# Four combinations of a scaled input: five GpSimd operations in place of four VectorE operations, in four gated stages

## The chip, the cores and the metric

The kernel runs on one core of one Trainium2 chip. The metric is the device time of one execution in microseconds. The kernel before took 2028.01 us (median of 3 runs, 2027.89 to 2028.39).

## The reference, cut to what matters

The program is two transformer blocks in float32 over 512 tokens of width 1024. The first has a SwiGLU feed-forward, a mixer (window attention beside a pooling branch) and a second SwiGLU. The second block has two layers, each a mixer followed by a convolutional feed-forward. The change touches only the first half (gate and up projections) of the four feed-forwards:

```
h = h + 0.5 * swiglu(rms_norm(h, g), w_gate, w_up, w_down)    # twice: stages up1, up2
u, v = split(rms_norm(h, w) @ w_up)                           # twice: stages up3, up4
c = conv_b + sum_j conv_w[j] * shift(u, 2 - j)
y = (gelu(c) * v) @ w_down
```

Each of these projections is 1024 by 2 x 2816.

## The kernel before, in words

Activations are kept with features on the 128 partitions and the 512 tokens along the free axis; `h` is 8 chunks of 128x512. Every float32 matrix product is made of three TensorE matmuls (`product`, L1285 to L1287): each factor is split into a rounded part (`hi`) and the remainder (`lo`), and hi*hi, hi*lo and lo*hi are summed in PSUM. ScalarE makes the `hi` parts by a copy (L1766 for weights, L1994 for weights of a summed pair, L2030 for `xq`), VectorE the `lo` parts by a subtraction (L1794, L2598).

A stage up1 to up4 works through 22 pairs of weight tiles (f = 0 to 21), each pair a gate tile and an up tile, double-buffered in `raw`, `w_hi` and `w_lo`. The first PLAIN = 6 pairs are computed plainly, 48 matmuls of 512 columns each. From f = 6 on each product is put together from seven products of halved size, a Strassen-like scheme, which takes sums of the weight quarters (`w_sum`, L2535 to L2545) and seven combinations of the quarters of the scaled input: `xq`, seven pieces of 128x1024 float32 for the values and seven for their `hi` parts. This input has to be ready when pair 6 begins. It is made while VectorE also evacuates the plain pairs:

- `scaled_quarters` (L2580, after pair 1): eight instructions of VectorE, 128x512 each, write the four quarters x11, x21, x12, x22 = h * norm weight * rstd.
- `sum_quarters`: four instructions of VectorE on 128x1024. Part 0 (L2588, L2589) makes s1 = x22 - x21 and s2 = -s1 - x11, part 1 (L2591, L2592) overwrites x21 by x11 - x21 and makes s4 = -x12 - s2. The last one raises `xq_sum`. In up1 and up2 all four follow `scaled_quarters` at once; in up3 and up4 part 0 stands in pair 2 behind the convolution taps (L2606, L2609) and part 1 in pair 3 ahead of that pair's `rest_weights`.
- `round_quarters` (ScalarE, L2030) waits for `xq_sum`. Its group 0 stands in ScalarE's order of pair 3 behind the weights of pair 5 and ahead of `silu(3)`, group 1 behind `silu(3)`, groups 2 and 3 in pair 4.
- `rest_quarters` (VectorE, L2598): group 0 at the end of pair 3, groups 1 and 2 in pair 4, group 3 in pair 5. TensorE waits for each in pair 6 (`xq_ready`, L1576 to L1595).

Each engine executes its own instructions in the order in which they are written. VectorE's order in pair f (`plain_dve`) is: evacuate gate and up from PSUM (L2666 or L2669, and L2670), weights' remainder of pair f + 2 (L1794), in up3 and up4 the taps, the product with the activated gate (L2564), which waits for ScalarE's `silu`, and then what belongs to the special pairs. Pair 3 ends with the weight sums of pair 6 and `rest_quarters(0)`. TensorE can start pair f only when pair f - 2 is evacuated and the weights of f are split.

GpSimd's program (L3003 on) has nothing to compute in up1 and up2. In up3 and up4 it issues the transfers that add up weight quarters: `copy_gate` (L3036) for pair 6 early in the stage, then for each pair from 6 on the accumulating transfers L3027 (waits for the pair's weights) and L3029 (waits for the copy).

Of the kernel before, what the change touches and what calls it, by code (L numbers as in the profile page):

```python
# [9 lines left out]
ALU = mybir.AluOpType  # L10
# [23 lines left out]
SEVEN = ("up1", "up2", "up3", "up4")  # L34
# [106 lines left out]
def wait(eng, sem, count):  # L141

    if not isinstance(count, int) or count > 0:
        eng.wait_ge(sem, count)


def chunk(t, m, width=T):

    if isinstance(m, int):
        return t[:, m * width:(m + 1) * width]  # L150
    return t[:, bass.ds(m * width, width)]


def column(t, c):
    return t[:, c:c + 1] if isinstance(c, int) else t[:, bass.ds(c, 1)]
# [18 lines left out]
def build(nc, x_t, vecs, weights, mixer_consts, pool_tab, small_consts, pool_w, sinks, rel_bias, out_t, scratch, skew, stop=None):  # L174
# [4 lines left out]
    with ExitStack() as ctx:  # L179
# [4 lines left out]
        def at(name, shape, dt, offset):  # L184
            return nc.alloc_sbuf_tensor_at(name, shape, dt, offset=offset)
# [6 lines left out]
        def sem(name):  # L192
            return ctx.enter_context(nc.semaphore(name))
# [48 lines left out]
        xq32 = at("xq32", [P, 14 * XQ], F32, act_at + 32 * ROOM)  # L242
# [151 lines left out]
        hg_turned = sem("hg_turned")  # L394
        hg_gated = sem("hg_gated")
        xq_sum, xq_hi_ready, xq_ready = sem("xq_sum"), sem("xq_hi_ready"), sem("xq_ready")
        seven_done = sem("seven_done")
        seven_kept = sem("seven_kept")
        w_summed = sem("w_summed")
# [729 lines left out]
        def own_act(f):  # L1129
            return chunk(act32, (16 + f) % KF)  # L1130
# [7 lines left out]
        def quad(t, n, count=1):  # L1138
            return t[:, n * QUAD:(n + count) * QUAD]
# [4 lines left out]
        def xq_lo_at(n, count=1):  # L1144
            return slice((7 + n) * XQ, (7 + n + count) * XQ)
# [642 lines left out]
        def rest_weights(eng, q, i, per):  # L1788

            slot = q % 2  # L1790
            wait(eng, hi_rounded, whole_rounds(q) + per * i)
            n = PAIR_TILES[q] * P
            w = slice(slot * PAIR, slot * PAIR + n)
            eng.tensor_tensor(w_lo[:, w], raw[:, w], w_hi[:, w].bitcast(F32), ALU.subtract).then_inc(lo_rounded, 1)  # L1794
# [477 lines left out]
        def _(eng):  # L2272
            steps = [0]

            def link(ins):

                steps[0] += 1
                ins.then_inc(dve_step, 1)
                eng.wait_ge(dve_step, steps[0])
# [267 lines left out]
            def rest_sum(st, f, c):  # L2547

                eng.wait_ge(w_sum_hi_ready, 3 * seven_index(st, f) + c + 1)
                eng.tensor_tensor(quad(w_sum_lo, c), sum_at(st, f, c), quad(w_sum_hi, c).bitcast(F32), ALU.subtract)\  # L2550
                    .then_inc(w_sum_lo_ready, 1)
# [21 lines left out]
            def scaled_quarters(st):  # L2573

                for k in range(KD):
                    own = chunk(h, k).rearrange("p (a t) -> p a t", a=2)
                    by = rstd[:, :].rearrange("p (a t) -> p a t", a=2)
                    c, j = 2 * (k // 4), k % 4
                    to = xq32[:, xq_lo_at(c, 2)].rearrange("p (a k t) -> p a k t", a=2, k=KD // 2)[:, :, j, :]
                    ins = eng.scalar_tensor_tensor(to, own, column(vec, SEVEN_NORM[SEVEN.index(st.name)] + k), by,  # L2580
                                                   ALU.mult, ALU.mult)
                link(ins)

            def sum_quarters(st, part):

                x11, x21, x12, x22, s2, s1, s4 = (xq32[:, xq_lo_at(c)] for c in range(7))
                if part == 0:
                    link(eng.tensor_tensor(s1, x22, x21, ALU.subtract))  # L2588
                    link(eng.scalar_tensor_tensor(s2, s1, -1.0, x11, ALU.mult, ALU.subtract))  # L2589
                else:  # L2590
                    eng.tensor_tensor(x21, x11, x21, ALU.subtract)  # L2591
                    eng.scalar_tensor_tensor(s4, x12, -1.0, s2, ALU.mult, ALU.subtract).then_inc(xq_sum, 1)  # L2592

            def rest_quarters(st, j):

# [63 lines left out]
            def plain_dve(st, f, f0):  # L2659

                conv = st.evac == "conv"
                b = 5 if f == 0 else 2 * ((st.g0 + f) % 2)
                eng.wait_ge(pair_done, st.q0 + f + 1)
                if conv:
                    wait(eng, gate_ready, f0 + f)
                    eng.tensor_tensor(shifted[:, 2:], bank(b), rstd[:, :], ALU.mult).then_inc(u_ready, 1)  # L2666
                else:
                    wait(eng, gated_ready, f0 + f)
                    eng.tensor_tensor(gate[:, :], bank(b), rstd[:, :], ALU.mult).then_inc(gate_ready, 1)  # L2669
                eng.tensor_tensor(own_act(f), bank(b + 1), rstd[:, :], ALU.mult).then_inc(evacuated, 1)  # L2670
                if f == 3 and conv:
                    sum_quarters(st, 1)
                if 0 < f < PLAIN - 2:
                    rest_weights(eng, st.q0 + f + 2, 0, 0)
                if f == PLAIN - 2:
                    rest_weights(eng, st.q0 + PLAIN, 0, 0)
                    rest_sum(st, PLAIN, 0)
                if f == 1:
                    gated_product(st, 0, f0)
                if conv and f < PLAIN - 1:  # L2680
                    other_taps(st, f)
                if f == 1:
                    scaled_quarters(st)
                    if not conv:
                        sum_quarters(st, 0)
                        sum_quarters(st, 1)
                if f == 2 and conv:
                    sum_quarters(st, 0)
                if f == PLAIN - 2:
                    rest_quarters(st, 1)  # L2690
                if 0 < f < PLAIN - 1:
                    gated_product(st, f, f0)
                if f == PLAIN - 3:
                    sum_pair(st, PLAIN)
                    fourth_sum(st, PLAIN)
                    rest_quarters(st, 0)
                if f == PLAIN - 2:
                    rest_quarters(st, 2)
                    rest_sum(st, PLAIN, 1)
                if f == PLAIN - 1:  # L2700
                    rest_quarters(st, 3)
                    rest_sum(st, PLAIN, 2)
# [72 lines left out]
            for st in stages:  # L2775
                if st.name in IN:
                    a = IN.index(st.name)
# [47 lines left out]
                if st.name in OUT:  # L2825
                    a = OUT.index(st.name)
# [177 lines left out]
        def _(eng):  # L3004
# [30 lines left out]
            def copy_gate(st, f):  # L3035
                eng.dma_start(sum_at(st, f, 1), quad(weights[st.name][f], 0)).then_inc(copy_landed[f % 2], 16)  # L3036

            for st in stages:
                if st.name in ("up3", "up4"):
                    for f in range(PLAIN, KF):  # L3040
                        sums_by_transfer(st, f)
                if st.name == "in3":
                    eng.wait_ge(pair_done, st.q0)
                    eng.dma_start(mask3[:, :], mixer_consts[2][:, 2 * T:2 * T + P]).then_inc(const_landed, 16)
                    stream_gpsimd(eng)
                if st.name in IN:

                    eng.wait_ge(pair_done, st.q0)
                    a = IN.index(st.name)
                    eng.dma_start(mconst[:, :], mixer_consts[a]).then_inc(const_landed, 16)  # L3050
                    if a == 0:
                        eng.memset(swapped[:, :], 0.0).then_inc(swap_clear, 1)
                        eng.dma_start(ptab[:, :], pool_tab).then_inc(tab_landed, 16)
                        eng.dma_start(pw[:, :], pool_w).then_inc(tab_landed, 16)
                if st.name == "in1":
                    pool_gpsimd(eng)
                if st.name in HALVED and BARRIERS[st.name]["kind"] == "post":
                    bar, n = BARRIERS[st.name], HALVED.index(st.name)
                    tail = bar["x_index"] is None
                    for hf, m in tiles_in_order(st):  # L3060
                        if tail and (m % 2 if hf else m % 3 == 2):
                            continue
                        if hf:
                            eng.wait_ge(scaled_ready, bar["h0"] - 8 + m + 1)
                        else:
                            eng.wait_ge(a_scaled, KD * (n - 1) + m + 1)
                        own = half_chunk(h, m, hf)
                        done = tail_pool if tail else h_ready if hf else a_h
                        eng.tensor_tensor(own, own, (tail_product(m, hf) if tail else (gate, gated)[m % 2])[:, cols(hf)], ALU.add)\
                            .then_inc(done, 1)  # L3070
# [115 lines left out]
```

## Time and profile before

| what | value |
|---|---|
| median of 3 runs | 2028.01 us |
| the profiled execution's own time | 2028.04 us |
| its span, first to last instruction | 2026.3 us |
| TensorE busy | 2005.3 us, 99% |
| VectorE busy | 1459.0 us, 72% |
| ScalarE busy | 986.8 us, 49% |
| GpSimd busy | 244.1 us, 12% |
| granted TensorE clock | full in every slice |

The profile comes from one execution. Shares are of the span; a stage is seen in the timeline, where each row has a start, a duration, the engine, line, operation, output and inputs. In brackets stands how long the engine had been idle before the instruction, and what ended that.

### The profile page before, as it was taken

Reading aid. Unit: us, or ns where it says so; the run is one execution under the profiler, and the core shown is the slowest. Engines: PE = TensorE matmul, PEld = TensorE weight load, DVE = VectorE, ACT = ScalarE, POOL = GpSimd, SP = SyncE. Lnnn points to the kernel's source line nnn. Section 1 sums busy time; section 2 is a strip of 40 time slices with the busy share of each in tenths; the row PEclk is TensorE's granted clock in tenths of the full one; section 3 lists DMA queues with packets and bytes.
Section 4 is the critical chain, followed back from the end, with each engine's and each line's share of the span. In section 5 each row is a group of like instructions: output and inputs, shape, how many; then the busy total and the mean of one; then the engine's idle time right before and its main releaser. Section 6 shows DMA issues by size and latency. Waiting matters only on the chain.

```text
span 2026.3 us, 32634 instructions
## 1 busy us (share of the span) xinstructions
PE 2005.3 (99%) x12670; PEld 1757.3 (87%) x12670; DVE 1459.0 (72%) x2427; ACT 986.8 (49%) x1607; POOL 244.1 (12%) x266
## 2 busy tenths in 40 slices
PE   9999999999999999999999999999999999999998
PEld 7899988778899988988788899988877788999887
DVE  7888833786798863587778988933657779988733
ACT  5555622254445552453455555622557754555522
POOL 0000000500000000000002122000536520221001
PEclk9999999999999999999999999999999999999999
DMA  8322233312223223321321566333256624666232
GB/s 257 125 105 105 79 101 112 132 56 93 86 105 105 99 87 98 106 104 63 94 84 68 164 185 182 105 102 112 106 136 172 162 73 135 172 183 172 87 99 70
DMA packets 90141, 236.99 MB, mean 117 GB/s; under 512 B 47728, under 2 KB 51104, under 8 KB 73616
## 3 DMA queue, kind: packets, MB, share of 16 engines
q1 hardware_dynamic: 72896, 184.04, 27.6%
q0 software_dynamic: 14768, 37.49, 8.4%
q10 hardware_dynamic: 2336, 13.52, 1.9%
q8 instruction: 96, 1.57, 0.3%
q14 instruction: 45, 0.37, 0.1%
HBM read 211.86 MB, written 7.38 MB: 108 GB/s over the span
## 4 chain that ended last, share of the span: by engine, by line
PE 90%; DVE 6%; ACT 1%; issue 1%; DMA 0%; POOL 0%; SPq 0%; DVEq 0%
PE ps L1285 29%; PE ps L1286 28%; PE ps L1287 28%; DVE act L2556 1%; PE ps L512 1%; PE ps L525 1%; PE ps L736 1%; PE ps L718 1%; DVE w_lo L1784 1%; PE ps L703 1%; DVE w_lo L1794 1%; DVE w_sum_lo L2550 0%; DMA raw<-in_w_up 0%; PE ps L1272 0%; PE ps L1307 0%
## 5 line engine op out<-in xcount | busy, mean ns | idle before, releaser
L1794 DVE TENSOR_TENSOR w_lo<-raw,w_hi 128x2048 fp32r<-128x2048 f32 (+3 forms) x144 | 287.6, 1997 | 154.3 <-ACT w_hi L1766 146.3
L1285 PE MATMUL ps<-act,w_hi 128*128 128x512 f32 (+1 forms) x1026 | 376.3, 367 | 2.7 <-DVE w_lo L1794 1.6
L1286 PE MATMUL ps<-act,w_hi 128*128 128x512 f32 (+1 forms) x1026 | 372.0, 363 | 0.0
L1287 PE MATMUL ps<-act,w_lo 128*128 128x512 f32 (+1 forms) x1026 | 371.9, 362 | 0.0
L1285 PE MATMUL ps<-xq,w_hi 128*128 128x256 f32 x1024 | 290.6, 284 | 2.9 <-DVE up L2731 1.6
L1287 PE MATMUL ps<-xq,w_lo 128*128 128x256 f32 x1024 | 289.9, 283 | 0.0
L1286 PE MATMUL ps<-xq,w_hi 128*128 128x256 f32 x1024 | 289.9, 283 | 0.0
L1285 PEld LDWEIGHTS ps<-act,w_hi 128*128 128x128 f32 x1026 | 193.5, 189 | 40.4 <-issue 7.9
L1285 PE MATMUL ps<-xq,w_sum_hi 128*128 128x256 f32 x768 | 218.0, 284 | 1.7 <-ACT prod L2010 1.2
L1287 PEld LDWEIGHTS ps<-act,w_lo 128*128 128x128 f32 x1026 | 193.6, 189 | 30.0
L1286 PEld LDWEIGHTS ps<-act,w_hi 128*128 128x128 f32 x1026 | 193.7, 189 | 28.9
L1286 PE MATMUL ps<-xq,w_sum_hi 128*128 128x256 f32 x768 | 217.4, 283 | 0.0
L1287 PE MATMUL ps<-xq,w_sum_lo 128*128 128x256 f32 x768 | 217.4, 283 | 0.0
L1285 PEld LDWEIGHTS ps<-xq,w_hi 128*128 128x128 f32 x1024 | 196.6, 192 | 4.3 <-DVE up L2731 2.0
L1766 ACT ACTIVATE w_hi<-raw 128x1536 fp32r<-128x1536 f32 (+3 forms) x80 | 119.1, 1489 | 163.6 <-PE ps L1287 159.3
L1286 PEld LDWEIGHTS ps<-xq,w_hi 128*128 128x128 f32 x1024 | 196.6, 192 | 0.2
L1287 PEld LDWEIGHTS ps<-xq,w_lo 128*128 128x128 f32 x1024 | 196.6, 192 | 0.0
L1285 PE MATMUL ps<-x_split,w_hi 128*128 128x512 f32 (+1 forms) x400 | 161.3, 403 | 0.0
L1287 PE MATMUL ps<-x_split,w_lo 128*128 128x512 f32 (+1 forms) x400 | 153.0, 383 | 0.0
L1286 PE MATMUL ps<-x_split,w_hi 128*128 128x512 f32 (+1 forms) x400 | 152.9, 382 | 0.0
L1285 PEld LDWEIGHTS ps<-xq,w_sum_hi 128*128 128x128 f32 x768 | 147.4, 192 | 2.6 <-ACT prod L2010 1.6
L1287 PEld LDWEIGHTS ps<-xq,w_sum_lo 128*128 128x128 f32 x768 | 147.5, 192 | 0.0
(301 smaller groups left out, 3977.3 us busy)
## 6 DMA issues: line engine op xcount, KB each, us to landing
raw<-in_w_up SPq DMA_DIRECT2D x87, 1024.0 KB, 4.8
raw<-in_w_down SPq DMA_DIRECT2D x29, 768.0 KB, 4.2
raw<-in_w_in SPq DMA_DIRECT2D x20, 1024.0 KB, 4.7
raw<-in_w_down SPq DMA_DIRECT2D x29, 640.0 KB, 3.8
raw<-in_w_out SPq DMA_DIRECT2D x8, 1024.0 KB, 4.8
w_sum<-in_w_up POOLq DMA_DIRECT2D x32, 256.0 KB, 4.4
raw<-raw POOLq DMA_DIRECT2D x32, 256.0 KB, 3.3
w_sum_odd<-in_w_up POOLq DMA_DIRECT2D x32, 256.0 KB, 4.3
```

Source lines behind the costliest of these rows:

```text
L512: ins = pe.matmul(score_bank(i, hh)[:, at_:at_ + w], ring[rows, qs:qs + P], ring[rows, ks:ks + w], start=True, stop=True)
L525: ins = pe.matmul(pair_bank(c)[64 * hh:64 * hh + 64, n * P:(n + 1) * P], v_tok[:, vc:vc + 64], turned_at(u)[:, hh, at_ + j * P:at_ + (j + ...
L703: ins = pe.transpose(bank(TURN_BANK + hh)[:, to:to + P], exps_at(a, u, hh)[:, at_ + j * P:at_ + (j + 1) * P], ident)
L718: ins = pe.matmul(bank(SCORE_BANK + hh)[:, to:to + w], tile_at(a, ROPED[a][1 + c])[rows, n * P:(n + 1) * P], keys[rows, lo * P:(hi + 1) * ...
L736: ins = pe.matmul(pair_bank(c)[64 * hh:64 * hh + 64, n * P:(n + 1) * P], g_vtok[a][:, vc:vc + 64], g_turned_at(a, u)[:, hh, to:to + P], st ...
L1285: pe.matmul(own, hi, rhs_hi, start=start, stop=False, skip_group_check=more)
L1286: pe.matmul(own, hi, rhs_lo, start=False, stop=False, skip_group_check=more)
L1287: return pe.matmul(own, lo, rhs_hi, start=False, stop=stop, skip_group_check=more)
L1766: eng.activation(w_hi[:, w], raw[:, w], ACT.Copy).then_inc(hi_rounded, 1)
L1784: ins = eng.tensor_tensor(w_lo[:, w], raw[:, w], w_hi[:, w].bitcast(F32), ALU.subtract)
L1794: eng.tensor_tensor(w_lo[:, w], raw[:, w], w_hi[:, w].bitcast(F32), ALU.subtract).then_inc(lo_rounded, 1)
L2556: eng.tensor_tensor(chunk(act, act_lo(f)), own_act(f), chunk(act, act_hi(f)).bitcast(F32), ALU.subtract)\
```

## The change

`sum_quarters` leaves VectorE and becomes GpSimd's. The algebra is rearranged: s1 = x22 - x21, s4 = s1 + x11, x21 = x11 - x21, s2 = -s4, s4 = s4 - x12, five instructions on 128x1024 where there were four. Two semaphores are new: `xq_scaled`, raised by the last of the eight scaling instructions, which GpSimd waits for, and `xq_step`, which orders its own five. `xq_sum` is raised by the last as before, so ScalarE's waits are unchanged. In GpSimd's program the five stand ahead of the transfers of up3 and up4.

```diff
@@ scaled_quarters, sum_quarters (VectorE)
-                link(ins)
-
-            def sum_quarters(st, part):
-
-                x11, x21, x12, x22, s2, s1, s4 = (xq32[:, xq_lo_at(c)] for c in range(7))
-                if part == 0:
-                    link(eng.tensor_tensor(s1, x22, x21, ALU.subtract))
-                    link(eng.scalar_tensor_tensor(s2, s1, -1.0, x11, ALU.mult, ALU.subtract))
-                else:
-                    eng.tensor_tensor(x21, x11, x21, ALU.subtract)
-                    eng.scalar_tensor_tensor(s4, x12, -1.0, s2, ALU.mult, ALU.subtract).then_inc(xq_sum, 1)
+                ins.then_inc(xq_scaled, 1)
@@ plain_dve (VectorE)
-                if f == 3 and conv:
-                    sum_quarters(st, 1)
...
-                    if not conv:
-                        sum_quarters(st, 0)
-                        sum_quarters(st, 1)
-                if f == 2 and conv:
-                    sum_quarters(st, 0)
@@ the GpSimd program
+            def sum_quarters(st):
+
+                a = SEVEN.index(st.name)
+                x11, x21, x12, x22, s2, s1, s4 = (xq32[:, xq_lo_at(c)] for c in range(7))
+                eng.wait_ge(xq_scaled, a + 1)
+                eng.tensor_tensor(s1, x22, x21, ALU.subtract).then_inc(xq_step, 1)
+                eng.wait_ge(xq_step, 3 * a + 1)
+                eng.tensor_tensor(s4, s1, x11, ALU.add).then_inc(xq_step, 1)
+                eng.tensor_tensor(x21, x11, x21, ALU.subtract)
+                eng.wait_ge(xq_step, 3 * a + 2)
+                eng.tensor_scalar(s2, s4, -1.0, None, ALU.mult).then_inc(xq_step, 1)
+                eng.wait_ge(xq_step, 3 * a + 3)
+                eng.tensor_tensor(s4, s4, x12, ALU.subtract).then_inc(xq_sum, 1)
+
             for st in stages:
+                if st.name in SEVEN:
+                    sum_quarters(st)
                 if st.name in ("up3", "up4"):
                     for f in range(PLAIN, KF):
                         sums_by_transfer(st, f)
```

## Rows read from the trace of the kernel before

**Rows 1.** The page's first part: engine, busy us, share of the span, instructions.
```profile
PE 2005.3 (99%) x12670; PEld 1757.3 (87%) x12670; DVE 1459.0 (72%) x2427; ACT 986.8 (49%) x1607; POOL 244.1 (12%) x266
```
**Rows 2.** Timeline of TensorE in pair 6 and 7: start us, us, engine, line.
```profile
82.68 0.39 PE L1285 MATMUL ps<-xq,w_sum_hi 128*128 128x256 f32 x1 [0.59 <-ACT prod L2010]
1151.44 0.36 PE L1285 MATMUL ps<-xq,w_hi 128*128 128x256 f32 x1 [0.59 <-DVE w_lo L1794]
1157.67 0.39 PE L1285 MATMUL ps<-xq,w_sum_hi 128*128 128x256 f32 x1 [0.25 <-ACT up L2010]
1160.99 0.39 PE L1285 MATMUL ps<-xq,w_hi 128*128 128x256 f32 x1 [0.20 <-DVE up L2640]
1738.50 0.36 PE L1285 MATMUL ps<-xq,w_hi 128*128 128x256 f32 x1 [0.39 <-DVE w_lo L1794]
```
**Rows 3.** One line's instructions, minimum, median, maximum ns, first and last start.
```profile
L2588 DVE TENSOR_TENSOR xq<-xq x4: 1217/1222/1226, 43.5 to 1703.5; 128x1024 f32<-128x1024 f32 x4
```
**Rows 4.** Timeline of VectorE in up1.
```profile
38.10 5.38 DVE L2580 SCALAR_TENSOR_TENSOR xq<-h,vec,rstd 128x512 f32<-128x512 f32 x8
...
55.19 2.29 DVE L1794 TENSOR_TENSOR w_lo<-raw,w_hi 128x2048 fp32r<-128x2048 f32 x1 [0.72 <-ACT w_hi L1766]
...
59.57 0.69 DVE L2535 TENSOR_TENSOR w_sum<-raw 128x512 f32<-128x512 f32 x1 [1.36 <-DMA raw<-in_w_up]
...
74.94 0.69 DVE L2669 TENSOR_TENSOR gate<-ps,rstd 128x512 f32<-128x512 f32 x1 [0.37 <-PE ps L1287]
```
**Rows 5.** Timeline of ScalarE in up1.
```profile
55.06 1.90 ACT L2030 ACTIVATE xq<-xq 128x2048 fp32r<-128x2048 f32 x1
```
**Rows 6.** Timeline of VectorE in up2.
```profile
524.86 5.38 DVE L2580 SCALAR_TENSOR_TENSOR xq<-h,vec,rstd 128x512 f32<-128x512 f32 x8
...
543.81 2.29 DVE L1794 TENSOR_TENSOR w_lo<-raw,w_hi 128x2048 fp32r<-128x2048 f32 x1 [0.72 <-ACT w_hi L1766]
...
563.56 0.69 DVE L2669 TENSOR_TENSOR gate<-ps,rstd 128x512 f32<-128x512 f32 x1 [0.36 <-PE ps L1287]
```
**Rows 7.** Timeline of VectorE in up3.
```profile
1105.55 5.39 DVE L2580 SCALAR_TENSOR_TENSOR xq<-h,vec,rstd 128x512 f32<-128x512 f32 x8
...
1112.78 2.28 DVE L1794 TENSOR_TENSOR w_lo<-raw,w_hi 128x2048 fp32r<-128x2048 f32 x1
...
1127.44 0.69 DVE L2564 TENSOR_TENSOR act<-gated,act 128x512 f32<-128x512 f32 x1 [0.70 <-ACT gated L1983]
```
**Rows 8.** GpSimd's lines with SBUF inputs: minimum, median, maximum ns.
```profile
L3069 POOL TENSOR_TENSOR h<-h,gate x29: 720/915/1010, 1061.8 to 2019.2; 128x256 f32<-128x256 f32 x29
...
L424 POOL TENSOR_TENSOR pool_e<-csum x4: 1039/1288/1537, 369.2 to 388.8; 128x513 f32<-128x513 f32 x4
...
L427 POOL TENSOR_TENSOR pool_e<-pool_e,ptab x4: 1293/1306/1630, 370.3 to 390.4; 128x513 f32<-128x513 f32 x4
...
L630 POOL TENSOR_SCALAR biases<-biases x16: 1487/1650/2317, 1450.0 to 1597.2; 128x512 f32<-128x512 f32 x16
```
**Rows 9.** Timeline where GpSimd and VectorE compute side by side.
```profile
393.69 1.62 POOL L431 TENSOR_TENSOR proj<-gated,proj 128x512 f32<-128x512 f32 x1
394.08 1.78 DVE L828 TENSOR_TENSOR up<-proj,mconst 128x512 f32<-128x512 f32 x1
...
399.00 0.68 DVE L828 TENSOR_TENSOR up<-proj,mconst 128x512 f32<-128x512 f32 x1
...
1457.79 1.49 POOL L630 TENSOR_SCALAR biases<-biases 128x512 f32<-128x512 f32 x1 [1.89 <-DMA biases<-skew]
...
1458.52 0.69 DVE L1784 TENSOR_TENSOR w_lo<-raw,w_hi 128x512 fp32r<-128x512 f32 x1
```
**Rows 10.** Timeline of GpSimd in up3.
```profile
1091.22 0.58 POOL L3036 DMA_DIRECT2D w_sum<-in_w_up  x1 [8.45 <-DVE ssum L2471]
1120.31 0.91 POOL L3027 DMA_DIRECT2D raw<-raw  x1 [28.51 <-DMA raw<-in_w_up]
```

More of the change, by code:

```diff
@@ L396, in build @@
         xq_sum, xq_hi_ready, xq_ready = sem("xq_sum"), sem("xq_hi_ready"), sem("xq_ready")
+        xq_scaled, xq_step = sem("xq_scaled"), sem("xq_step")
         seven_done = sem("seven_done")
```

## The prediction

> **What bounds the kernel now.** I read the page first, then TensorE's timeline through the four stages, then the other engines' timelines around each hole in it. TensorE is busy 99% of the span [rows 1]: nothing is gained except where it idles, and every microsecond that something else makes it wait is added whole. Up to the start of pair 6 its matmuls in these stages stand back to back apart from the statistics at the start. The holes come in pairs 6 and 7, where the seven-product scheme begins. In up1 TensorE waits at 82.68 for a copy of ScalarE (0.59 us in the row, and a second hole of like size follows at 85.16; up2 has the same two). In up3 it waits three times, 0.59, 0.25 and 0.20 us, first for the weights' remainder of VectorE; in up4 the first is 0.39 and the other two are as in up3 [rows 2].
>
> What feeds these holes differs. In up1 VectorE is idle now and then before pair 6: 0.72 us at 55.19, 1.36 at 59.57, and at 74.94 it takes up the evacuation of pair 5 the moment TensorE has finished it, after 0.37 us of nothing to do [rows 4]. The chain to the hole starts at that evacuation, so what VectorE does before 74.94 is off the path. In up2 it is the same at 563.56, 0.36 us idle [rows 6]. In up3 (and up4) VectorE runs without a break from its scaling instructions to pair 7 except for 0.70 us at 1127.44 [rows 7], and the hole at 1151.44 names it. There its work is on the path.
>
> **The change part by part.** Taken off VectorE: four instructions of 1.22 us [rows 3] (the other three lines are alike), 4.9 us a stage. In up1 and up2 this only lengthens the idle time above: worth 0. In up3 and up4 it is worth at most the holes: the three waits come to 1.04 and 0.84 us, and each restart costs some 0.15 us more than the usual pitch (the first matmul after a wait is 0.36 to 0.39 us long where its neighbours are 0.28), so 1.5 and 1.3 us, 2.8 in all.
>
> Added to GpSimd: four tensor_tensor and one tensor_scalar on 128x1024. The trace has none of that size. tensor_tensor takes 0.72 us at 256 elements and 1.29 at 513, at the least [rows 8]; 0.57 us per 257 elements more gives 2.42 us at 1024. The lower bound is 2.0 (L424's fastest, 1.04 us for 513 elements [rows 8]), the upper 3.3 (twice the 1.63 maximum of L427); I take 2.42, since contended rows carry waiting that I count separately. tensor_scalar took 1.49 at 512 [rows 8], so 2.9. With 0.08 us from one to the next, the chain alone takes 4 x 2.42 + 2.9 + 0.3 = 12.9 us against 4.9 on VectorE. The Trainium skill, GPSIMD Engine Reference, section 3.1 (Elementwise), has 4497 ns for a tensor_tensor add of 2048, which would be an estimate of 2.25 us here. Its section 4.1 calls one-input operations roughly line-rate; the 1.49 us of rows 8 speaks against that for tensor_scalar, and by the page the chain would be some 2 us shorter.
>
> The price that decides is a different one: VectorE and GpSimd are not independent. At 394.08 VectorE's L828, two SBUF inputs, takes 1.78 us where the same instruction takes 0.68 at 399.00. GpSimd's L431 ran from 393.69 to 395.31; VectorE's ends at 395.86, 0.55 after it. So it did not move until GpSimd was through [rows 9]. An instruction of VectorE with one SBUF input, such as the evacuations from PSUM, keeps its 0.68 beside GpSimd. With tensor_scalar the wait is shorter: L630 ran 1457.79 to 1459.28, and L1784, begun 0.73 us into it, took its usual 0.69 [rows 9]. So I count a hold over the whole 2.42 us of a tensor_tensor and over half, 1.5 us, of the tensor_scalar. The Trainium skill, SBUF — State Buffer, "Who interferes with whom", says so too: the second read interface is shared, and whoever starts first has it for the whole instruction. By that rule in full the tensor_scalar would hold VectorE for 2.9 us, about 1 us more in a stage; the L630 row disagrees.
>
> What VectorE has to do meanwhile is nearly all of two SBUF inputs: weights' remainder (2.2 us), products (0.6), taps (0.75 each). I let the two alternate, whoever waits going next.
>
> Up1, walked: scaling ends 43.48 [rows 4]. Product of pair 1 to 44.1; GpSimd's first to 46.5, over two evacuations of VectorE (to 45.3), then VectorE stands 1.2 us; remainder of pair 4, 46.5 to 48.7; GpSimd's second 48.7 to 51.1; product of pair 2 to 51.7; third to 54.1; tensor_scalar 54.2 to 57.1, holding to 55.7; the remainder of pair 5, due at 55.19, runs 55.7 to 57.9; fifth 57.9 to 60.3. So `xq_sum` comes at T = 60.3, where ScalarE wants it at 55.06 [rows 5], and behind this wait stands `silu(3)`, for which VectorE's product of pair 3 waits. From T on: rounding 1.8 (1.90 in the row less its overlap with the next [rows 5]), silu 0.6, product 0.6, T + 3.0 for the weight sums. From them to the evacuation of pair 5 it was 74.94 - 59.57 - 0.37 = 15.0 us without slack [rows 4]. So VectorE reaches it at T + 18.0 = 78.3, and it was at 74.94: 3.4 us late, and with it the chain to the holes. T up to 56.9 would be free.
>
> Up2: scaling ends 530.24 [rows 6], pair by pair 1.9 us earlier relative to TensorE than in up1. Fourth operation ends 544.0, but VectorE takes the remainder of pair 5 at 543.81 to 546.0, and the fifth runs to 548.4. Free would be 563.56 - 18.0 = 545.6: 2.8 us late. Were GpSimd 0.3 us earlier, its fifth would go first and the cost be 0.6.
>
> Up3: scaling ends 1110.94 [rows 7]. Product to 1111.6; first GpSimd operation to 1114.0; remainder of pair 4 (at 1112.78 before) 1114.0 to 1116.2; second to 1118.6; tap L2606 to 1119.3; third to 1121.7; tap L2609 to 1122.4; tensor_scalar holds to 1123.9; product of pair 2 to 1124.5; evacuations to 1125.7; fifth 1125.4 to 1127.8; remainder of pair 5 1127.8 to 1130.0, just when TensorE comes to pair 5; taps to 1131.5, silu, product of pair 3 at 1132.2. It was at 1127.44 [rows 7]: VectorE stood 9.6 us and saved 4.9. It has no slack until pair 7, so TensorE is 4.7 us late. Up4 has the same order and the same naming of VectorE at the hole: 4.7.
>
> GpSimd's queue: `copy_gate` of pair 6 moves from 1091.22 [rows 10] to 1127.8, behind the five; the transfer at 1120.31 becomes 1128.4. Landing takes 3.3 us for the latter and 4.4 for the former (the page's sixth part), so the pair is summed at about 1132.6, when VectorE is ready for it at 1132.8, and L3029 follows at 1132.8 and lands by about 1138; ScalarE uses it before `silu(4)`, whose gate is ready at about 1141. Cost 0; with that cover gone, as long as it is late. In up1 and up2 nothing is queued behind.
>
> **Sum** against the profiled execution (span 2026.3, own time 2028.04, as good as the median 2028.01): 3.4 + 2.8 + 4.7 + 4.7 = 15.6, 2043.6 us. With 2.0 us per tensor_tensor, each stage keeps some 1.6 us: 1.8, 0, 3.1, 3.1, so 2036. If GpSimd keeps the port between its second, third and fourth operations, which have no real wait between them, the walks give 1.8, 0, 5.2, 5.2, so 2040. With 2.8 us, half way to the upper bound, up1 and up2 cost 5 each and up3 and up4 6.3, so 2051.
>
> **The rivals.** *No holding*: VectorE keeps its rates beside GpSimd. Then `xq_sum` comes at 43.5 + 12.9 = 56.4 and 543.1, both free, and up3 and up4 gain the holes: 2028.0 - 2.8 = 2025.2. This is the other side; it decides by whether a two-input instruction of VectorE next to one of GpSimd stays at its usual length. For it: in up1 and up2 the room is there. Against it: L828 and its like. *Half holding*: tensor_tensor too frees the port half way, as L630 did. VectorE stands about 4.9 us, as much as it saved, in up3 and up4; up1 costs 1 to 2: 2030. Against it: L828 waited to within 0.15 us of GpSimd's end. *The queue*: the transfers behind the five land late for ScalarE in up3 and up4, if each takes 8 us instead of 4.4; up to 3 us a stage more, 2049. Against it: 3 us of room.
>
> **How the numbers follow.** The forecast has 0.73, its own range 2036 to 2051; half holding 0.12, no holding 0.07, the queue 0.08. What can be told from no change is 0.2%, 4.1 us. No holding counts mostly as the same (2025.2), a third of it as faster; of half holding 0.10 is the same; and the low end of the forecast adds little. Faster 0.03, same 0.14, slower 0.83. Range 2031 to 2051.
>
> **What would show it.** Five GpSimd instructions after each scaling, 2.4 us or a little over, the fourth nearer 2.9. L1794, L2564, L2606 and L2609 of pairs 2 and 3 long by up to 2.4 us beside them, L2666 to L2670 unchanged. ScalarE's L2030 idle before it for about 5 us in up1 and up2, released by GpSimd. The evacuation of pair 5 about 3 us later than TensorE is done with it; first TensorE hole of up3 of some 5 us. It would be wrong if those VectorE instructions kept 2.28 and 0.68, or if L2030 found `xq_sum` ready.

## The result and the profile after

The changed kernel takes 2045.37 us (median of 4 runs, 2043.55 to 2046.21) against 2028.20 for the one before in the same measurement: ratio 1.0084, 95% interval 1.0072 to 1.0095. That is 17 us slower; 2043.6 had been forecast. The profiled execution took 2046.21 us, span 2044.4.

The page's first part, as in [rows 1], and its chain that ended last:

```profile
PE 2011.3 (98%) x12670; PEld 1760.4 (86%) x12670; DVE 1462.7 (72%) x2411; ACT 986.2 (48%) x1607; POOL 311.3 (15%) x286
...
PE 82%; DVE 10%; POOL 3%; DMA 2%; issue 2%; ACT 1%; SPq 0%; DVEq 0%; ACTq 0%
```

The chain of the kernel before:

```profile
PE 90%; DVE 6%; ACT 1%; issue 1%; DMA 0%; POOL 0%; SPq 0%; DVEq 0%
```

The number to see is VectorE's. Sixteen instructions of 1.22 us have left it, 19.5 us, and its busy time has risen from 1459.0 to 1462.7: what it saved it spends being held, and a held instruction counts as busy. GpSimd is busy 67 us more, and of the chain of work that ended last it now holds 3%, DMA 2% and VectorE 10%, where they held 0, 0 and 6%.

To see which stage lost what, I compare the start of `scaled_quarters` in each stage, an instruction that stands at the same place of the program in every variant. Timeline of VectorE of the changed kernel, the four starts:

```profile
38.10 5.38 DVE L2581 SCALAR_TENSOR_TENSOR xq<-h,vec,rstd 128x512 f32<-128x512 f32 x8
...
528.97 5.38 DVE L2581 SCALAR_TENSOR_TENSOR xq<-h,vec,rstd 128x512 f32<-128x512 f32 x8
...
1109.80 5.38 DVE L2581 SCALAR_TENSOR_TENSOR xq<-h,vec,rstd 128x512 f32<-128x512 f32 x8
...
1704.26 5.38 DVE L2581 SCALAR_TENSOR_TENSOR xq<-h,vec,rstd 128x512 f32<-128x512 f32 x8
```

Before they were at 38.10, 524.86, 1105.55 [rows 4, 6, 7], and for up4:

```profile
1692.62 5.38 DVE L2580 SCALAR_TENSOR_TENSOR xq<-h,vec,rstd 128x512 f32<-128x512 f32 x8
```

A stretch runs from one start to the next, the last to the end of the span. Growth: up1 4.1 us, up2 0.1, up3 7.4, up4 6.5, together 18.1, which is the difference of the spans. Forecast were 3.4, 2.8, 4.7 and 4.7. A stretch holds everything up to the next start, and where a run changes nothing it still moves by up to 0.3 us (first_two_only in up3, last_two_only in up2, below). So for up3 and up4 I also use a nearer mark, the last of TensorE's restarts in pair 7, in the kernel before at 1160.99 [rows 2] and 1748.06, both 55.4 us behind the start of their stage. TensorE of the changed kernel:

```profile
1171.77 0.39 PE L1286 MATMUL ps<-xq,w_hi 128*128 128x256 f32 x1 [0.20 <-DVE up L2631]
...
1766.22 0.39 PE L1286 MATMUL ps<-xq,w_hi 128*128 128x256 f32 x1 [0.20 <-DVE up L2631]
```

That is 62.0 us behind the start in both: both stages are 6.5 us late by pair 7, and the other 0.9 us of up3's 7.4 comes later; TensorE has two short waits there, at 1240.2 and 1243.5, that the kernel before does not have.

**GpSimd and VectorE in up3**, GpSimd's timeline without its third operation, with the transfers that it issues behind; then VectorE's in the same stretch:

```profile
1115.27 2.79 POOL L3027 TENSOR_TENSOR xq<-xq 128x1024 f32<-128x1024 f32 x1 [28.24 <-DVE xq L2581]
1118.13 4.32 POOL L3029 TENSOR_TENSOR xq<-xq 128x1024 f32<-128x1024 f32 x1
...
1125.23 3.21 POOL L3032 TENSOR_SCALAR xq<-xq 128x1024 f32<-128x1024 f32 x1
1128.52 4.37 POOL L3034 TENSOR_TENSOR xq<-xq 128x1024 f32<-128x1024 f32 x1
1132.84 0.61 POOL L3020 DMA_DIRECT2D w_sum<-in_w_up  x1
1133.45 0.95 POOL L3011 DMA_DIRECT2D raw<-raw  x1
```

```profile
1116.91 3.29 DVE L1795 TENSOR_TENSOR w_lo<-raw,w_hi 128x2048 fp32r<-128x2048 f32 x1
1120.12 2.88 DVE L2597 SCALAR_TENSOR_TENSOR gate<-shifted,vec,gate 128x512 f32<-128x512 f32 x1
1123.04 2.77 DVE L2600 SCALAR_TENSOR_TENSOR gate<-shifted,vec,gate 128x512 f32<-128x512 f32 x1
1126.50 0.74 DVE L2565 TENSOR_TENSOR act<-gated,act 128x512 f32<-128x512 f32 x1 [0.70 <-ACT gated L1984]
...
1130.57 2.88 DVE L2597 SCALAR_TENSOR_TENSOR gate<-shifted,vec,gate 128x512 f32<-128x512 f32 x1
...
1135.40 0.69 DVE L2565 TENSOR_TENSOR act<-gated,act 128x512 f32<-128x512 f32 x1 [1.17 <-ACT gated L1984]
1138.80 0.69 DVE L2540 TENSOR_TENSOR w_sum<-raw 128x512 f32<-128x512 f32 x1 [2.71 <-DMA raw<-raw]
```

Read the two together. A tap of 0.75 us takes 2.88 and 2.77, the remainder 3.29 instead of 2.28: each ends its own length after the GpSimd instruction that was running when it came up. And it goes both ways: GpSimd's second operation takes 4.32 us, because VectorE's remainder has the port from 1117.9 to 1120.2. Four VectorE instructions in these rows stood 1.0, 2.1, 2.0 and 2.1 us. The product at 1126.50, wholly beside the tensor_scalar, took 0.74: that operation held it for 0.05 us and not for the 1.5 us of the walk. So VectorE stood 7.3 us and not 9.6. With 4.9 us saved and 1.2 us more of waiting for ScalarE's `silu` (0.70 and 1.17 us idle, where it was 0.70 once), the product of pair 3 comes at 1135.40, 3.7 us late by the start of the stage. The last row is one that the walk did not have: 2.71 us idle for a transfer. Together 3.7 and 2.7 make 6.4 of the 6.5 us at pair 7.

**Up1**: ScalarE waits for GpSimd, VectorE behind it, and then TensorE. Timelines of GpSimd, ScalarE, VectorE and TensorE:

```profile
46.44 4.32 POOL L3029 TENSOR_TENSOR xq<-xq 128x1024 f32<-128x1024 f32 x1
...
56.40 3.34 POOL L3034 TENSOR_TENSOR xq<-xq 128x1024 f32<-128x1024 f32 x1
```

```profile
59.77 1.92 ACT L2031 ACTIVATE xq<-xq 128x2048 fp32r<-128x2048 f32 x1 [4.61 <-POOL xq L3034]
```

```profile
62.24 0.69 DVE L2565 TENSOR_TENSOR act<-gated,act 128x512 f32<-128x512 f32 x1 [4.75 <-ACT gated L1984]
...
77.43 0.69 DVE L2660 TENSOR_TENSOR gate<-ps,rstd 128x512 f32<-128x512 f32 x1
```

```profile
85.17 0.58 PE L1286 MATMUL ps<-xq,w_sum_hi 128*128 128x256 f32 x1 [3.07 <-ACT prod L2011]
85.55 0.41 PE L1287 MATMUL ps<-xq,w_sum_hi 128*128 128x256 f32 x1
```

`xq_sum` came at 59.7. What counts here is that GpSimd was held: its four tensor_tensor took 2.79, 4.32, 2.84 and 3.34 us, 3.7 more than four of 2.39 (the length of the one in up2 that met nobody). Without that the sums would have been there at 56.0 (an estimate), before the 56.9 that the prediction calls free. The evacuation of pair 5 came at 77.43 instead of 74.94 [rows 4], 2.5 us late, and the hole of [rows 2] at 82.68 now ends at 85.17, again 2.5 later. The rest of the 4.1 us is the length of the matmuls behind it, 0.41 us instead of 0.28. The same execution by stretches of 4 us, TensorE alone (length, busy, granted clock, DMA share, GB/s):

```profile
80.00:84.00 4.00, 2.10 (x18) 1.00 0.00 0
84.00:88.00 4.00, 2.83 (x13) 0.55 0.05 8
88.00:92.00 4.00, 4.00 (x24) 0.59 0.64 254
92.00:96.00 4.00, 4.00 (x36) 1.00 0.00 0
```

After an idle stretch of 3.07 us the granted clock is at the 1.2 GHz level (0.55 and 0.59 as means of mixed stretches) until 91.2; it fell within the idle stretch. Some 28 matmuls come at a pitch of 0.21 instead of 0.12 us, 2.6 us in all; a second hole of about 1 us that the kernel before had at 85 is covered by that.

**Up2**: GpSimd's fifth operation began at 547.27, VectorE's remainder at 547.92, and it was VectorE that stood:

```profile
547.92 3.89 DVE L1795 TENSOR_TENSOR w_lo<-raw,w_hi 128x2048 fp32r<-128x2048 f32 x1 [0.73 <-ACT w_hi L1767]
...
567.66 0.69 DVE L2660 TENSOR_TENSOR gate<-ps,rstd 128x512 f32<-128x512 f32 x1 [0.22 <-PE ps L1288]
```

VectorE is still 0.22 us ahead of TensorE at pair 5, and the stage costs nothing.

### The profile page after: what moved, and what is told of

The parts are those of the page before. It is cut to its first block, busy times and chain, and to the rows that moved or that the text cites. A ratio compares the mean times of both kernels' runs of the same rounds, so it can differ in the third digit from the quotient of the medians.

```text
span 2044.4 us, 32638 instructions
## 1 busy us (share of the span) xinstructions
PE 2011.3 (98%) x12670; PEld 1760.4 (86%) x12670; DVE 1462.7 (72%) x2411; ACT 986.2 (48%) x1607; POOL 311.3 (15%) x286
## 4 chain that ended last, share of the span: by engine, by line
PE 82%; DVE 10%; POOL 3%; DMA 2%; issue 2%; ACT 1%; SPq 0%; DVEq 0%; ACTq 0%
PE ps L1286 26%; PE ps L1288 25%; PE ps L1287 25%; DVE w_lo L1795 1%; DVE act L2557 1%; PE ps L513 1%; PE ps L526 1%; DVE xq L2589 1%; DMA raw<-raw 1%; PE ps L737 1%; PE ps L719 1%; DMA raw<-in_w_up 1%; DVE xq L2581 1%; DVE w_lo L1785 1%; POOL xq L3029 1%
## 5 line engine op out<-in xcount | busy, mean ns | idle before, releaser
L1795 DVE TENSOR_TENSOR w_lo<-raw,w_hi 128x2048 fp32r<-128x2048 f32 (+3 forms) x144 | 292.4, 2031 | 154.1 <-ACT w_hi L1767 147.1
L1286 PEld LDWEIGHTS ps<-xq,w_sum_hi 128*128 128x128 f32 x768 | 147.9, 193 | 8.6 <-ACT prod L2011 4.1
L1287 PEld LDWEIGHTS ps<-xq,w_sum_hi 128*128 128x128 f32 x768 | 147.9, 193 | 0.0
```

The costliest lines, as they stand in the source:

```text
L1286: pe.matmul(own, hi, rhs_hi, start=start, stop=False, skip_group_check=more)
L1287: pe.matmul(own, hi, rhs_lo, start=False, stop=False, skip_group_check=more)
```

## The experiments

Loss by stage is the growth of each stretch against the kernel before, from the profile; the ratio is from the timed runs, with the kernel before at 2027.8 to 2028.3 beside them.

| kernel | us | ratio (95%) | up1 | up2 | up3 | up4 |
|---|---|---|---|---|---|---|
| changed | 2045.37 | 1.0084 (1.0072 to 1.0095) | 4.1 | 0.1 | 7.4 | 6.5 |
| beside_only | 2062.93 | 1.0172 (1.0155 to 1.0189) | 10.2 | 8.8 | 8.2 | 8.2 |
| delay_only | 2034.13 | 1.0032 (1.0019 to 1.0044) | 0.2 | 0.1 | 3.1 | 2.4 |
| delay_early | 2027.14 | 0.9994 (0.9985 to 1.0004) | 0.3 | 0.0 | -1.0 | -0.3 |
| transfers_early | 2038.15 | 1.0049 (1.0032 to 1.0066) | 3.5 | 0.0 | 3.3 | 3.7 |
| silu_first | 2034.61 | 1.0029 (1.0018 to 1.0040) | 0.3 | 0.0 | 3.0 | 3.3 |
| first_two_only | 2031.19 | 1.0014 (1.0005 to 1.0024) | 2.5 | 0.2 | -0.3 | 0.0 |
| last_two_only | 2041.48 | 1.0063 (1.0046 to 1.0079) | 0.1 | 0.3 | 6.2 | 7.0 |
| hole_filled | 2041.80 | 1.0067 (1.0050 to 1.0084) | 2.6 | 0.1 | 5.2 | 5.2 |
| one_operation | 2030.37 | 1.0013 (1.0003 to 1.0022) | 0.6 | 0.1 | 0.6 | 0.9 |

My theory was the held port: the two engines take turns when both read two SBUF operands. Its rival was that nothing is held and a chain of 13 us in place of one of 5 is simply late.

### Only the port, only the delay

**beside_only**: the kernel before, and GpSimd works beside it for nobody, from the seventh of the eight scaling instructions on. In up3 and up4 the copy for pair 6 is issued ahead of its five operations and the accumulating transfer (`third_gate`) between the fourth and the fifth.

```diff
+                eng.wait_ge(xq_scaled, a + 1)
+                for k in range(5):
+                    if k == 4 and st.name in ("up3", "up4"):
+                        third_gate(st, PLAIN)
+                    if k == 3:
+                        ins = eng.tensor_scalar(beside[:, :], h[:, 0:2 * QUAD], -1.0, None, ALU.mult)
+                    else:
+                        ins = eng.tensor_tensor(beside[:, :], h[:, 0:2 * QUAD], h[:, 2 * QUAD:4 * QUAD], ALU.add)
+                    ins.then_inc(xq_step, 1)
+                    eng.wait_ge(xq_step, 5 * a + k + 1)
```

> VectorE keeps its four sums as in the kernel before; GpSimd runs five instructions of the same kinds and sizes beside them, on h into a piece of memory that nobody reads, and the transfers of up3 and up4 are issued ahead of them, so nobody waits for GpSimd's result. Theory of the held port: VectorE is held as in the changed kernel (its L1794, L2564, L2606, L2609 of pairs 2 and 3 take up to 3 us) but saves nothing, so up3 and up4 lose about 8 us each (3.7 us of lag in the changed kernel plus the 4.9 that it had saved there), up1 and up2 some 2 to 5 each: about 2050 us. Theory that the loss is only the lateness of GpSimd's result: no one waits for it here, so 2028 us, same as before.

Measured: 2062.93 us, 35 us slower, though nobody waits for a result of GpSimd except the last reader of its memory. The nearly threefold length of VectorE's own sums in up1 is the plainest picture of it; its timeline, where the same lines took 1.22 us [rows 3]:

```profile
43.05 3.31 DVE L2592 TENSOR_TENSOR xq<-xq 128x1024 f32<-128x1024 f32 x1
46.40 3.30 DVE L2593 SCALAR_TENSOR_TENSOR xq<-xq 128x1024 f32<-128x1024 f32 x1
49.73 3.30 DVE L2595 TENSOR_TENSOR xq<-xq 128x1024 f32<-128x1024 f32 x1
```

The holding is shown, and the rival is out as a full account. The loss is not all holding, though. The total of 2062.93 is 13 us above the 2050 that I had expected, and up1 and up2 (10.2, 8.8) are well above my 2 to 5. VectorE is held three times for some 2.1 us and once for 0.8, so the four sums last 12.0 us in place of 4.9, and the remainder of pair 4 comes too late for TensorE to start pair 4:

```profile
60.30 0.80 PE L1287 MATMUL ps<-x_open,w_hi 128*128 128x512 f32 x1 [7.63 <-DVE w_lo L1796]
```

And in all four stages the granted clock fell to the 1.2 GHz level in such an idle stretch (7.63, 5.79, 3.73 and 3.58 us). Matmuls of 512 columns then come at a pitch of 0.43 instead of 0.23 us, which adds 2.2 us in up1, 2.8 in up2 and up to 1.7 each in up3 and up4. Up to some 8 of the 35 us are TensorE's clock.

The fourth of the sums, 2.05 us long, ran beside the tensor_scalar: held for 0.8 us. In up3 of the same run a tap beside the tensor_scalar took 1.41 us (held 0.7), and the sum that came up 1.8 us into it 1.21, its usual length. So a tensor_scalar of about 3 us holds VectorE in its first part at most, where a tensor_tensor holds it to its end.

**delay_only**: the opposite. GpSimd writes zeros for 11 us and reads nothing; the sums are left out.

```diff
-                eng.tensor_tensor(s1, x22, x21, ALU.subtract).then_inc(xq_step, 1)
...
-                eng.tensor_tensor(s4, s4, x12, ALU.subtract).then_inc(xq_sum, 1)
+                for k in range(11):
+                    eng.memset((s1, s2, s4)[k % 3], 0.0).then_inc(xq_step, 1)
+                    eng.wait_ge(xq_step, 11 * a + k + 1)
+                eng.memset(s4[:, 0:2], 0.0).then_inc(xq_sum, 1)
```

> The changed kernel with the five GpSimd operations replaced by twelve writes of zeros (memset) into the three pieces s1, s2, s4, about 13 us in a chain, so xq_sum comes about when an undisturbed chain would raise it; the sums themselves are left out. A memset reads nothing. Theory of the held port: VectorE keeps its usual 2.28 and 0.68 us beside it and has its 4.9 us saved; up1 and up2 cost nothing (T near 56.6 and 543), up3 and up4 lose at most 2 us each because the silu of pair 3 and the transfers still stand behind the chain: 2025 to 2032 us. Theory that an undisturbed but slower chain explains the loss: still above 2040 us.

Measured: 2034.13, above the 2025 to 2032 that I gave, up1 and up2 free as expected. VectorE kept its lengths beside the memsets. The timeline of VectorE in up3:

```profile
1112.71 2.29 DVE L1795 TENSOR_TENSOR w_lo<-raw,w_hi 128x2048 fp32r<-128x2048 f32 x1
1114.91 0.76 DVE L2597 SCALAR_TENSOR_TENSOR gate<-shifted,vec,gate 128x512 f32<-128x512 f32 x1
...
1131.41 0.69 DVE L2540 TENSOR_TENSOR w_sum<-raw 128x512 f32<-128x512 f32 x1 [5.22 <-DMA raw<-raw]
```

So a GpSimd instruction that writes only does not hold VectorE, and there is a second loss in up3 and up4 that has nothing to do with the port: 5.22 us idle for the transfer L3011, which GpSimd had issued at 1123.04, behind its chain. It landed 8.3 us later; before, its median was 3.3 us. The kernel's own load of 1 MB began at 1123.53 beside it and landed after 7.6 us instead of 4.8: that they slowed each other fits, and is not shown by a run of its own. One caution on this run: the chain of memsets was 11.2 us long, 2 us less than intended, so it bounds the cost of mere lateness in up1 and up2 from below only.

### The transfers behind the chain

**transfers_early** issues the copy ahead of the five operations, and L3011 between the fourth and fifth (the lines that take both out of their old place are left out here).

```diff
+                if st.name in ("up3", "up4"):
+                    eng.wait_ge(ssum_ready, KD * (st.stat + 1))
+                    copy_gate(st, PLAIN)
                 if st.name in SEVEN:
                     sum_quarters(st)
@@ sum_quarters
+                if st.name in ("up3", "up4"):
+                    third_gate(st, PLAIN)
                 eng.wait_ge(xq_step, 3 * a + 3)
```

> The changed kernel, but in up3 and up4 GpSimd issues the copy for pair 6 before its five operations and the accumulating transfer L3011 between the fourth and the fifth. If the 2.7 us that VectorE waits for that transfer in up3 (and in up4) are part of the loss: 2 to 3 us less in each of the two stages, 2040 us. If VectorE's held port alone sets the end there (the transfer only names itself last): within 1 us of the changed kernel's 2045.

Measured: 2038.15, 7 us better than the change. Up3 fell from 7.4 to 3.3, up4 from 6.5 to 3.7; at the mark in pair 7 both stages are 3.7 late instead of 6.5, and the difference of 2.8 matches the 2.7 us that VectorE had been idle for the transfer, which landed after 3.4 us in this run. VectorE's L2540 now follows the product at once:

```profile
1134.23 0.69 DVE L2565 TENSOR_TENSOR act<-gated,act 128x512 f32<-128x512 f32 x1 [1.17 <-ACT gated L1984]
1134.84 0.68 DVE L2540 TENSOR_TENSOR w_sum<-raw 128x512 f32<-128x512 f32 x1
```

**delay_early** combines that with delay_only: neither held nor behind the queue, and the sums left out.

```diff
@@ delay_only, with the transfers as in transfers_early
                 eng.memset(s4[:, 0:2], 0.0).then_inc(xq_sum, 1)
+                if st.name in ("up3", "up4"):
+                    third_gate(st, PLAIN)
```

> delay_only (sums left out, GpSimd writes zeros instead) with GpSimd's transfers moved as in transfers_early. There up3 and up4 lost 3.05 and 2.4 us although VectorE was never held, with VectorE idle 5.22 us before L2540 for the transfer L3011. If that wait was all of it: up3 and up4 now end no later than in the kernel before, or gain the 1.3 to 1.5 us of their holes: 2025 to 2028 us. If the four operations' place on VectorE had cost nothing and something else in up3 and up4 is late: still 2032 or more.

Measured: 2027.14, ratio 0.9994, no change that can be told. At the mark in pair 7 up3 is 0.7 and up4 0.4 us early, of the 2.8 us that I had put on the holes of the kernel before: the first hole of each stage is gone, and the other two stand as they were, 0.26 and 0.20 us. With the two causes out nothing is left of the loss, and next to nothing was there to be gained: freeing VectorE of all four sums, at no cost elsewhere, is worth 1 us by the profile, less than the timed runs can tell.

### Which stages

**first_two_only** and **last_two_only** leave the sums on VectorE in up3 and up4, or in up1 and up2.

```diff
-                if st.name in SEVEN:
+                if st.name in ("up1", "up2"):      # last_two_only: ("up3", "up4")
                     sum_quarters(st)
```

> Only up1 and up2 use GpSimd; up3 and up4 are as in the kernel before. In the changed kernel up1 took 4.11 us longer (2.5 us of lateness, the rest TensorE's clock after the 3.35 us hole) and up2 0.14: 2032.4 us if the stages' losses add up. Prediction's walk: 2028.1 + 3.4 + 2.8 = 2034.3.

> Only up3 and up4 use GpSimd. In the changed kernel's trace they took 7.4 and 6.5 us longer: 2042 us if the stages' losses add up. Prediction's walk: 2028.1 + 4.7 + 4.7 = 2037.5.

Measured: 2031.19 (2030.02 to 2033.07) and 2041.48. They were expected at 2032.4 and 2042. Their losses, 2.9 and 13.2 us, add up to 16.2, and the changed kernel's is 17.2: to within 1 us the stages are independent. In first_two_only up1 lost 2.5 us, not 4.1, because in its profiled execution the clock did not fall. It had the same hole, 3.07 us idle, and yet:

```profile
84.45 0.39 PE L1286 MATMUL ps<-xq,w_sum_hi 128*128 128x256 f32 x1 [3.07 <-ACT prod L2011]
```

```profile
84.00:88.00 4.00, 2.76 (x21) 1.00 0.17 33
88.00:92.00 4.00, 4.00 (x36) 1.00 0.54 229
```

This was the fastest of its ten timed executions, 2030.02 of up to 2033.07 us, so the others may not all have kept the clock.

### Up1: the wait in front of silu, and the clock

**silu_first** is transfers_early with ScalarE's first rounding of `xq` moved behind `silu(3)`.

```diff
-                if f == PLAIN - 3:
-                    round_quarters(a, 0)
...
                 if f == PLAIN - 3:
-                    round_quarters(a, 1)
+                    round_quarters(a, 0, 1)
```

> transfers_early with ScalarE's round_quarters group 0 moved behind silu(3), so that the product of pair 3 no longer stands behind GpSimd's result. If up1's loss (3.5 us in transfers_early) is the wait for xq_sum in front of silu(3): it falls to 0 to 1 us, and VectorE's product of pair 3 in up1 comes at 57.5 again instead of 62.2; up3 and up4 gain at most 0.5 us each, since the held port keeps VectorE behind there: about 2034 us. If the held port delays up1 too: no more than 1 us less than transfers_early's 2038.2.

Measured: 2034.61. Up1 lost 0.3 us instead of 3.5, so its loss was the wait in ScalarE's order. The product of pair 3 began at 57.26 and was held to 60.1 by GpSimd's fifth operation, which the room in this stage swallowed. Up3 and up4 stay at 3.0 and 3.3: that is the held port with the transfers and ScalarE's order out of the way. Of the versions with the sums of all four stages on GpSimd it is the fastest, and it is still slower than the kernel before.

**hole_filled** is the changed kernel with 24 matmuls into an unused PSUM bank in pair 6 of up1.

```diff
+                if f == PLAIN and st.name == "up1":
+                    for _ in range(24):
+                        pe.matmul(bank(WARM_BANK)[:, 0:HALF], tile_of(w_hi, slot, 0), xq[:, 0:HALF], start=True, stop=True)
                 pe.wait_ge(seven_kept, 3 * n + 3)
```

> The changed kernel with 24 more matmuls of 256 columns into an unused PSUM bank in pair 6 of up1, where TensorE idled 3.35 us. In the changed kernel the granted clock then fell to its 1.2 GHz level from 86 to 91 us and up1 ended 4.1 us later than before. If the idle stretch is what the clock answers: the granted clock stays at 2.4 GHz there, and up2 starts 1 to 2 us earlier than in the changed kernel (VectorE's scaling in up2 at 527 to 528 instead of 528.97), in all 2044 us. If the clock falls whatever TensorE does there: up2's scaling starts at 528.9 or later.

Measured: 2041.80, 2 us below the 2044 expected, and up1 at 2.6 us with the granted clock at 1.00 throughout that stage. Up1 is what I expected, but it does not prove what I wanted, since first_two_only kept its clock with the hole unfilled and has the same 2.5. What can be said: with the hole open the clock fell in the changed kernel and in transfers_early and not in first_two_only. That the filling keeps it up is not shown.

Up3 and up4, where nothing was edited, came out at 5.2 instead of 7.4 and 6.5. GpSimd issued L3014 (L3011 of the changed kernel) at 1131.84, and VectorE had it here:

```profile
1136.14 0.69 DVE L2543 TENSOR_TENSOR w_sum<-raw 128x512 f32<-128x512 f32 x1 [1.66 <-DMA raw<-raw]
```

It landed after 4.2 us, in up4 after 3.9, where it took 5.3 in both stages of the changed kernel, and that is the difference: 1.1 and 1.3 us at the mark in pair 7. Yet the 1 MB load had been issued 2.6 us ahead of it in both kernels. So how long it takes at this place is not settled by the load beside it. And in up3 of this run the clock fell, after an idle stretch of 2.55 us:

```profile
1150.27 0.58 PE L1286 MATMUL ps<-xq,w_sum_hi 128*128 128x256 f32 x1 [0.48 <-DVE xq L2592]
```

```profile
1148.00:1152.00 4.00, 3.52 (x19) 0.57 0.00 0
1152.00:1156.00 4.00, 4.00 (x35) 1.00 0.60 135
```

That cost nothing to be seen: the next two holes, 1.12 and 0.83 us in the changed kernel, shrank to 0.48 and 0.37.

### One operation

**one_operation** moves only x21 = x11 - x21.

```diff
-                    eng.tensor_tensor(x21, x11, x21, ALU.subtract)
@@ the GpSimd program
+                eng.wait_ge(xq_scaled, SEVEN.index(st.name) + 1)
+                eng.tensor_tensor(x21, x11, x21, ALU.subtract).then_inc(xq_sum, 1)
```

> The kernel before with a single one of the four sums moved to GpSimd in each stage: x21 = x11 - x21, after s1 is made; the copy for pair 6 stays early in the stage. VectorE saves 1.14 us and meets one GpSimd operation of 2.4 us. Theory of the held port, in proportion: VectorE is held once, for up to 2.4 us less what it does from PSUM in that time, so up3 and up4 lose 0.5 to 1.2 us each, up1 and up2 nothing: 2029 to 2030.5 us, within what can be told from no change. Theory that the loss comes from the chain of five alone: 2026 to 2028 us.

Measured: 2030.37 us, ratio 1.0013, within what was expected, though up1 lost 0.6 us where I had put nothing (a TensorE hole of 0.25 us at 52.99, waiting for VectorE). VectorE saves 1.14 us and in up3 its product, 0.69 us long, takes 2.79:

```profile
1119.22 2.79 DVE L2565 TENSOR_TENSOR act<-gated,act 128x512 f32<-128x512 f32 x1
```

One operation moved costs 2.1 us of waiting for 1.14 saved, and up3 and up4 are both 1.0 us late at the mark in pair 7, which is the difference.

## Why the prediction was right, step by step

The direction and the sum were right, 15.6 us forecast and 17.2 measured, and the main mechanism is shown by beside_only against delay_only. The terms are another matter: of four only one was close, and up2, 2.7 too high, offset more than half of up3 and up4, together 4.5 too low. That the sum came so near is in part luck.

*Length of the operations.* 2.42 us was taken for a tensor_tensor; where it met nobody, in up2, the fifth took 2.39 us. The tensor_scalar took 2.77 to 3.21 for 2.9. Extending from the shortest rows, and not from means that hold waiting, was right. The estimate of 2.25 us from the Trainium skill, GPSIMD Engine Reference, section 3.1, is close too; its section 4.1, one-input operations at roughly line-rate, is contradicted by 2.77 us for 1024 elements, for which VectorE takes 1.22.

*The held port.* Right in kind, and in size for tensor_tensor: 1.0, 2.1, 2.0 and 2.1 us in up3. For tensor_scalar it was too much: 1.5 us were counted, and VectorE stood 0.05 us beside it in up3 of the changed kernel and 0.8 and 0.7 in beside_only. GpSimd did not keep the port between its second and third operation either, the case priced at 2040. From delay_only it is new that GpSimd's writes do not hold: a memset beside VectorE left it at 2.29 and 0.76. The Trainium skill, SBUF — State Buffer, "Who interferes with whom", says that an instruction of GpSimd which only writes does not contend with two SBUF inputs; the trace agrees.

*Up1.* 3.4 forecast, 2.5 us of lateness measured: `xq_sum` came at T = 59.7 and not 60.3, and 17.7 us stood between T and pair 5, not 18.0. The remaining 1.6 is the clock, which the walk did not have.

*Up2.* 2.8 forecast, 0.1 measured. The step that failed is who goes first at 543.8 in the walk. GpSimd's fifth operation went first, by 0.65 us. Its tensor_scalar, which the walk has end at 544.0, ended at 547.19, which is 543.1 by the clock of the walk (4.1 us earlier). The prediction named this outcome, at a cost of 0.6. An order that near should have been given half the weight, not a remark.

*Up3 and up4.* 4.7 each forecast, 7.4 and 6.5 measured, 6.5 and 6.5 at pair 7. Two steps failed, one each way. The holding alone is 3.7 and not 4.7, in the changed kernel up to the product of pair 3 and in transfers_early at pair 7; the tensor_scalar is what was too much. And "Cost 0" for GpSimd's queue was 2.8: the transfer was taken to land 3.3 us after issue, its median in the kernel before. It landed 5.3 us after issue, 2.7 us after VectorE was ready. It then ran beside the 1 MB load and the copy, but hole_filled had it after 4.2 and 3.9 us beside the same two, so what sets its time is open. The rival *the queue* was thus partly true together with the forecast. It had been priced at up to 3 us a stage and given 0.08, as if it excluded the forecast; the two add.

*The gain.* 2.8 us were put on the holes in up3 and up4. With everything else out of the way they gave 1.1 (delay_early, at pair 7): of the three holes only the first went away.

## What to carry to other kernels

Before moving elementwise work from VectorE to GpSimd, list what VectorE does meanwhile: if it reads two SBUF operands, the engines take turns, and each 1.2 us moved cost it about 2 us of standing here. It costs VectorE nothing only where VectorE idles, where it reads PSUM (the evacuation at 44.01 kept its 0.68 us beside GpSimd's first operation), or where GpSimd only writes. Where the port is contended, GpSimd's own result comes later too, as in up1. Look too at what stands behind the result on every queue: here a ScalarE instruction order cost 3 us and GpSimd's own transfers 3 us a stage. Both were had back by reordering; no version here had the port's share back. And a median landing time of a transfer holds for its old time of issue only.

## What the runs showed of the hardware that I had not expected

- TensorE's granted clock fell to 1.2 GHz in a hole of 3.07 us in up1 and stayed there for about 6 us of work, at a cost of up to 2.6 us. With the same 3.07 us it fell in two of three profiled executions. It fell in all four holes of 3.58 to 7.63 us (beside_only). Of five profiled holes of 2.54 or 2.55 us in up3 and up4, with short holes and matmuls around them, it fell after one (up3 of hole_filled) and stayed at 2.4 after the others. So a hole of 2.5 to 3 us is a risk and not a rule. What tips it stays open.
- The holding is in turns and in both directions: of two engines that wait for each other, each goes after one instruction of the other. GpSimd's operations of 2.4 us lasted up to 4.37.
- A tensor_scalar of GpSimd does not hold VectorE as a tensor_tensor does: of about 3 us it cost a VectorE instruction with two SBUF inputs 0.05 to 0.8 us, and instructions begun later beside it nothing.
- The same accumulating transfer of 256 KB, issued by GpSimd, landed after 3.3 us (median before), 3.9 and 4.2 (hole_filled), 5.3 (changed) and 8.3 us (delay_only, up3). Other transfers were under way each time; which of them sets the time is not shown.

One of the holes after which the clock stayed up, TensorE in up3 of the changed kernel:

```profile
1150.12 0.39 PE L1286 MATMUL ps<-xq,w_hi 128*128 128x256 f32 x1 [2.54 <-DVE xq L2589]
```
